# The feed-forward operand of a two-block kernel, laid out as hi and lo side by side per k-tile

## The reference

```python
u = rms_norm(h, g_pre_mlp[l])
f = jnp.square(jax.nn.relu(u @ w_up[l])) @ w_down[l]     # 2048 -> 8192 -> 2048
h = h + rms_norm(f, g_post_mlp[l])
return h[:, N_META:]
```

## Time and profile before

| what | value |
|---|---|
| median of three runs | 2076.09 us |
| the profiled execution, its own time | 2077.31 us |
| its span, first to last instruction | 2075.3 us |
| mean granted TensorE clock | 0.998 |
| PE busy | 2028.3 us, 98% |
| weight loads busy (beside PE) | 1810.9 us, 87% |
| DVE busy | 1409.5 us, 68% |
| ACT busy | 926.9 us, 45% |
| DMA read from HBM | 458.85 MB, 222 GB/s over the span |

### The profile page before, as it was taken

How to read it: one execution, slowest core, us unless ns; L and a number is a source line. 1 busy time by engine, 2 the same in 40 slices (tenths; PEclk the granted TensorE clock), 3 DMA queues, 4 the chain that set the end, 5 groups by cost and what they waited for, 6 DMA issues and landing times.

```text
span 2075.3 us, 35011 instructions
## 1 busy us (share of the span) xinstructions
PE 2028.3 (98%) x13385; PEld 1810.9 (87%) x13385; DVE 1409.5 (68%) x1967; ACT 926.9 (45%) x1390; POOL 35.0 (2%) x69
## 2 busy tenths in 40 slices
PE   5999999999999999999999999999999999999998
PEld 2789998779999988999999998888888888888886
DVE  5458898785787768898997555566456556545655
ACT  3344455364635544434346334454344434434443
POOL 0000000000000000000000000000000000000000
PEclk9999999999999999999999999999999999999999
DMA  9988888955576663445445555545555555555553
GB/s 375 411 331 313 332 319 318 352 234 198 193 286 231 234 225 143 163 183 181 166 180 183 203 182 184 201 166 195 189 196 186 188 198 183 194 189 190 194 185 140
DMA packets 64404, 462.41 MB, mean 223 GB/s; under 512 B 7264, under 2 KB 7808, under 8 KB 8368
## 3 DMA queue, kind: packets, MB, share of 16 engines
q1 hardware_dynamic: 55712, 400.01, 52.0%
q0 software_dynamic: 8592, 61.00, 7.9%
HBM read 458.85 MB, written 2.13 MB: 222 GB/s over the span
## 4 chain that ended last, share of the span: by engine, by line
PE 69%; DVE 7%; ACT 2%; issue 1%; DVEq 0%; ACTq 0%
PE ps L564 17%; PE ps L565 17%; PE ps L566 17%; PE ps L581 11%; PE ps L582 6%; DVE w_lo L1780 2%; DVE area L1817 1%; DVE st L1800 1%; ACT w_hi L1228 0%; PE ps L612 0%; ACT sc L1485 0%; DVE X L2287 0%; ACT sc L1491 0%; DVE grow L2388 0%; DVE area L2388 0%
## 5 line engine op out<-in xcount | busy, mean ns | idle before, releaser
L1780 DVE TENSOR_TENSOR w_lo<-raw,w_hi 128x1024 fp32r<-128x1024 f32 (+1 forms) x642 | 753.7, 1205 | 369.6 <-ACT w_hi L1228 367.5
L1228 ACT CAST w_hi<-raw 128x1024 fp32r<-128x1024 f32 (+2 forms) x642 | 640.3, 1036 | 452.6 <-PE ps L566 451.7
L564 PE MATMUL ps<-a,w_lo 128*128 128x256 f32 (+1 forms) x1888 | 538.9, 285 | 4.0 <-DVE sc L2054 1.2
L565 PE MATMUL ps<-a,w_hi 128*128 128x256 f32 (+1 forms) x1888 | 534.1, 283 | 0.0
L566 PE MATMUL ps<-a,w_hi 128*128 128x256 f32 (+1 forms) x1888 | 533.0, 282 | 0.0
L564 PEld LDWEIGHTS ps<-a,w_lo 128*128 128x128 f32 x1888 | 356.4, 189 | 26.5 <-issue 23.8
L581 PE MATMUL ps<-a,w_hi 128*128 128x512 f32 x1024 | 358.7, 393 | 0.4 <-DVE a L1902 0.4
L566 PEld LDWEIGHTS ps<-a,w_hi 128*128 128x128 f32 x1888 | 356.4, 189 | 0.0
L565 PEld LDWEIGHTS ps<-a,w_hi 128*128 128x128 f32 x1888 | 355.0, 188 | 0.5 <-issue 0.5
L582 PE MATMUL ps<-a,w_lo 128*128 128x256 f32 x1024 | 287.1, 280 | 0.0
L564 PE MATMUL ps<-w_hi,y_lo 128*128 128x512 f32 x720 | 281.3, 391 | 0.0
(11 more groups left out here) (284 smaller groups left out, 2344.5 us busy)
## 6 DMA issues: line engine op xcount, KB each, us to landing
raw<-in_stream SPq DMA_DIRECT2D x331, 1024.0 KB, 4.8
area<-in_ada POOLq DMA_DIRECT2D x50, 1024.0 KB, 5.5
area<-in_ada SPq DMA_DIRECT2D x38, 1024.0 KB, 8.4
grow<-in_ada SPq DMA_DIRECT2D x8, 1024.0 KB, 7.3
area<-in_rows POOLq DMA_DIRECT2D x4, 1024.0 KB, 5.0
X<-in_x SPq DMA_DIRECT2D x1, 2048.0 KB, 8.9
grow<-row_scratch POOLq DMA_DIRECT2D x2, 1024.0 KB, 8.0
grow<-in_rows POOLq DMA_DIRECT2D x2, 1024.0 KB, 4.7
```

What stands on the lines that cost most here:

```text
L564: pe.matmul(o, w[1], a[0], start=first, stop=False, skip_group_check=shared)
L565: pe.matmul(o, w[0], a[1], start=False, stop=False, skip_group_check=shared)
L1228: ac.copy(to, raw[:, bass.ds((g % RAW) * CH + at, n)]).then_inc(hi_ready, 1)
L1780: ve.tensor_tensor(to, raw[:, bass.ds((g % RAW) * CH + at, n)], hi.bitcast(F32), ALU.subtract).then_inc(lo_ready, 1)
```

## The change

The feed-forward operand gets a layout of its own in the same tensor `a`. Tile k now takes 512 contiguous columns from column 512 * k, which is byte 2048 * k: 256 hi columns, then 256 lo columns. ACT and DVE write there when n is 3, and `mm_halves` reads there. The first matmul's moving operand is now one run of 512 columns, where it was two runs of 256 columns that lie 17408 bytes apart. The second's is the first half of that run. `FF_AT`, a number of columns by which the whole layout is displaced, is 0. Every other stage uses `a` as before. Each engine has the same instructions in the same order as before, with the same sizes and the same waits; only addresses and the steps of the operands differ.

```diff
+FF_AT = 0
...
+        def f_both(k, at=0, n=2 * T):
+
+            return a_both[:, FF_AT + 2 * T * k + at:FF_AT + 2 * T * k + at + n]
+
+        def hi_tile(n, k):
+
+            return f_both(k, 0, T) if n == 3 else a_tile(a_hi, k)
+
+        def lo_tile(n, k):
+
+            return f_both(k, T, T) if n == 3 else a_tile(a_lo, k)
...
             def mm_halves(b, w, k, first, last):
 
-                both = tiles(a_both[:, :], 2)[:, :, k * TM + META:(k + 1) * TM]
-                pe.matmul(tiles(bank(b, 0, 2 * T), 2), w[0], both, start=first, stop=False)
-                return pe.matmul(bank(b), w[1], a_tile(a_hi, k), start=False, stop=last)
+                pe.matmul(bank(b, 0, 2 * T), w[0], f_both(k), start=first, stop=False)
+                return pe.matmul(bank(b), w[1], f_both(k, 0, T), start=False, stop=last)
...
-                    ac.activation(a_tile(a_hi, m), turned_tile(n, m), ACT.Copy, scale=v(gain, m)).then_inc(fm_hi, 1)
+                    ac.activation(hi_tile(n, m), turned_tile(n, m), ACT.Copy, scale=v(gain, m)).then_inc(fm_hi, 1)
...
-                    o = ve.scalar_tensor_tensor(out=a_tile(a_lo, m), in0=turned_tile(n, m), scalar=v(gain, m),
-                                                in1=a_tile(a_hi, m).bitcast(F32), op0=ALU.mult, op1=ALU.subtract)
+                    o = ve.scalar_tensor_tensor(out=lo_tile(n, m), in0=turned_tile(n, m), scalar=v(gain, m),
+                                                in1=hi_tile(n, m).bitcast(F32), op0=ALU.mult, op1=ALU.subtract)
```

## The result

The changed kernel took 2083.18 us (median of 9 runs, 2079.53 to 2087.53); the one before took 2078.46 us (9 runs, the three known before among them, 2075.36 to 2081.43). The ratio is 1.0021, with a 95% interval of 1.0012 to 1.003. I had forecast 2.5 us less, with a range up to 2077.8 us. By the interval the change costs 2.5 to 6.2 us. In three of the four up stages it did the opposite of the forecast; in the first, in the execution profiled here, it did what I had forecast.

The account below looks back on a forecast made before the run. PE's own pace was taken to bound the kernel. A new pair of 226.8 + 119.9 = 346.7 ns, against 349.1, saves 2.5 us over 1024 pairs: 2076.09 - 2.5 = 2073.6 us, range 2069.0 to 2077.8.

Parts of the forecast that it names:

- What bounds the kernel: Whole kernel, up stages above all: PE's own pace sets the time, and nothing else is near to taking over.
- The sum of the new pair: Up stages: long plus short matmul take 346.7 ns, against 349.1; 2.5 us less over 1024 pairs.
- The old pair's parts: Up stages, old layout: the 349.1 ns pair split into 230.7 ns for 512 columns and 118.4 for 256.
- Bounds: All 1024 up-stage pairs as cheap as the cheapest old pair, 9.3 us saved; as dear as the dearest, 11.2 us lost.
- Writes and cover: ACT and DVE writes counted as nothing, at most 0.3 us at the opening; DVE's slack leaves no wait uncovered.
- The slower rival: Up stages: both operands at one remainder of 512 bytes make every pair 0.36 us, +11.2 us, 2087.3 us; chance 0.06.
- My sign for it: In the timeline of an up stage, a pair of 0.35 us or more would mean the even place costs.
- The faster rival: Up stages: short matmul keeps 118.4 ns, long falls to 226.8, pair 345.2 ns; 4.0 us saved, 2072.1 us; chance 0.22.
- The rival of no difference: Up stages: excess belongs to each matmul and its weight load, so layout changes nothing, 2076.1 us; chance 0.15.
- The rules weighed: SBUF reads: only crossing 16-byte lines costs, so the change does nothing; PE reads its two operands through separate ports.

Follow-up runs that it names:

- e6: Changed kernel, last up stage issuing each chunk's matmuls in different orders: long-short pairs 5.64 to 5.66 us a chunk, eight long then eight short 5.587 us.
- e3: Changed kernel with tiles 528 columns apart, each beginning 64 bytes further on within 2048: second up stage 89.36 us.
- e4: Changed kernel, but the first matmul reads two runs of 256 columns, all places multiples of 1024 bytes: second up stage 90.44 us.
- e12: Changed kernel, last up stage reading stationary tile and moving operand displaced by 0 to 64 and 0 to 48 columns: 5.549 to 5.661 us a chunk.
- e5: Changed kernel, last up stage reading the moving operand displaced by 0 to 112 columns: 5.612 to 5.657 us a chunk.
- e1: Changed kernel with extra matmuls or transposes before some chunks of the last up stage: undisturbed chunks took 5.65 to 5.66 us or 5.546 to 5.547 us.
- e8: Changed kernel with two matmuls exchanged in the second chunk of up stages 1 to 3: those stages 88.84 us, ratio to the kernel before 0.9996.

## Why the prediction was wrong

- **What bounds the kernel: right.** PE alone, no wait uncovered, nothing hidden. A change of 4 ns in a pair did reach the end in full (3 x 1.07 us lost and 0.6 won make the 2.6 us of the table).
- **The sum of the new pair: the step that failed.** "The new pair is 226.8 + 119.9 = 346.7 ns." Both terms came from stages in which all matmuls have one length. The down stage still runs at 226.8 next door, but a long matmul between short ones does not: in e6 it takes five of a kind to get there. The trace of the kernel before had shown it already, at the start of the down stage behind the second up stage (timeline of PE):

```profile
1626.43 0.40 PE L564 MATMUL ps<-w_hi,y_lo 128*128 128x512 f32 x1
...
1628.74 0.39 PE L565 MATMUL ps<-w_lo,y_hi 128*128 128x512 f32 x1
...
1631.01 0.39 PE L566 MATMUL ps<-w_hi,y_hi 128*128 128x512 f32 x1
```

  The first ten of them take 2.31 us, 231 ns each, and the next ten 2.27 us, 227 each: at the same places and with no short ones between, the pace isn't 226.8 from the start. In the slow rhythm the long one takes 241, 236 and 232 ns, 236 in the mean, and the short one 120, 113 and 118, 117 in the mean. The long one came out 9.5 ns dearer than its term, the short one 2.9 ns cheaper, and the pair was 353.3 ns over three stages. That 346.7 was met to the nanosecond by the quick rhythm is then partly luck: its terms are 232 and 115.
- **The old pair's parts: nearly right, but read wrongly.** The trace's means are 230.8 and 118.3, against 230.7 and 118.4. I took the 3.9 ns between 230.7 and 226.8 for the price of two runs and of moving places. e3 shows that the second run costs nothing, and e4 that even places cost more.
- **Bounds: right in size, unused.** The dearest pairs of the earlier trace rows would have given +11.2 us. The true pair, 353.3, lies between 349.1 and that. (By the exact starts the old pairs run from 344 to 358 ns; 340 and 360 came from rows rounded to 10 ns.)
- **Writes and cover: right as far as seen.** DVE's share of a stage is the same, 56.75 us. From the first pair to the beginning of the first window it took 7.66 us, against 7.58, inside the 0.3 us that I had allowed.
- **The rivals.** The slower rival came nearest: the even layout costs, and e12 shows that the reads of the two operands do matter to each other; that it is the fetch of the *next* weights isn't shown. Its condition, both operands at the same remainder, isn't what makes a pair dear: the quick rhythm has it too, and e5 met chunks as slow (5.65 us) with the operands 64 and 192 bytes off it. Its price was that of the dearest old pair, 360 ns, and I gave it 0.06 because the uniform stages seemed to refute it. They didn't, for the reason above. My sign for it, a pair of 0.35 us or more, is what the timeline shows. The faster rival (the short half stays at 118.4 or less) came true in its half and was of no use. The rival of no difference fell.
- **The rules weighed**, both of the Trainium skill, "SBUF — State Buffer". That only lines crossed count ("Door 1: The DMA port swizzle"): e3 bears out that a second run costs nothing, but e5 and e12 show places counting where runs are the same. That the two operands come through ports of their own ("Who interferes with whom"): it would leave e12 without any effect of how they lie to each other, and there is one of 0.04 us a chunk.
- **What I didn't consider** is that the time of such a loop isn't a sum of prices. With a layout that repeats exactly, PE falls into one of a few cycles, at 346.7 or 353.3 ns a pair, and keeps it. With one that moves on by 64 bytes per tile it goes through one cycle of eight pairs, however it was entered, and comes out at one mean, 349.1. A forecast for the new layout had to say which cycle each stage would enter, and I know of nothing in the profile before that tells it.

Left open: what in the chip joins the two reads, why the slow cycle has three pairs and the quick one two or one, and which of them an entry leads to. Each was found by trying. Whether `FF_AT` other than 0 would help in all four stages wasn't run as a kernel; e5 met no good place.

## What to carry to other kernels

Before pricing a matmul by another stage's pace, ask whether the mix of lengths is the same there; the first of a row, six to ten long ones here, cost several ns more or less than the settled pace. When a PE-bound loop is made perfectly regular in its addresses, look at the starts of single matmuls: a repeated pattern means a locked cycle, and exchanging two matmuls once may move it to a better one at no cost. Differences of this size are read from the time of a stage in the trace, since the times of whole runs of one kernel lay 3 to 8 us apart here, and the part before the change alone scattered by 3.5 us.

## What the runs showed of the hardware that I had not expected

- The same two matmuls at the same addresses, with no wait, ran at 346.7 or 353.3 ns a pair for a whole stage of 90 us, and which it was depended on what came before: one to three small extra matmuls (e1), two matmuls exchanged (e8), or how PE came out of a stall of some 100 ns (block 0).
- The pace of a matmul with 512 columns lay between 224 and 241 ns, of one with 256 between 112 and 124 ns, by the distance of the stationary from the moving operand within 256 bytes and by what came before (e5, e12).
- A moving operand in two runs of 256 columns, 17408 bytes apart, cost no more than one run of 512 (e3 against before: 89.36 and 89.37 us).
